# Building the scan's decay matrices by two fp32r products instead of a GpSimd mask and one fp32 product

## The chip, the core and the metric

One core of a Trainium2 chip runs the whole kernel as one program. The metric is device time in microseconds (us) of one execution; the figure of a kernel is the median of its runs. The engines are PE (matrix products), ACT (ScalarE), DVE (VectorE), POOL (GpSimd) and the DMA queue of SP, each with its own instruction stream, kept in step by semaphores.

## What is computed

The reference is one layer of a hybrid decoder for a 528-row prompt (16 meta tokens and 512) and 8 samples of 8 rows, 592 rows in all: a normalisation, one input projection, a Mamba-2 scan with 32 heads in 4 groups of 8, a short gated convolution, a merge, and a mixture of experts. The change lies in the scan. Within a chunk of rows, a head's weights are

```
acum  = cumsum(dt * a_neg)                       # running sum inside the chunk
seg   = acum[l] - acum[s]
decay = exp(where(s <= l, seg, -inf))
wts   = (C B^T)[l, s] * decay * dt[s]
y_diag = wts @ x
```

so each group, chunk and head needs a square matrix of differences of running sums, cut by the causal mask, through an exponential.

## The kernel before

The 592 rows are held as five tiles (`TILES`): four of 128 rows and a last one of 80, which holds the prompt's last 16 rows and the eight samples. The projections are products in fp32r of weights split into a high and a low part; `pe_block` (line 649) issues one 128-column block, either whole (48 products: 24 weight tiles, each times two column halves of 264 and 328) or one half at a time (`part`, 24 products). Each block's weights come through SP's queue (`load_block`, L478), are split by ACT (`split_hi`, L1656) and by POOL (`split_lo`, L1954).

The scan runs over four groups `g`. Every engine's order inside a group is written out by hand. First come the projections and convolutions of the group (DVE L1258 and L1260, ACT L1733 and L1734), then the five tiles `i`. In tile `i`, PE transposes x (L755), forms C B^T (L758) and B's transpose (L759), and makes two banks of decay exponents, `q` = 0 and 1, four heads each (L770). For these POOL has built `rbuf` ahead (`decays`, L2035): for each head the lower mask `m_le` times that tile's `da` column. One fp32 product of the strict mask `m_gt` with `rbuf` sums it up: column c of row s gets the sum of `da` over the rows between s and c. ACT takes the exponential of the whole bank (L1767), DVE multiplies by C B^T, which it has masked on the way out of PSUM (`cbm`, L1280; the product L1285), and PE uses the result at L822. L776 gives the contribution of the carried state, L828 the new state, L846 adds the former. Between the two banks of tiles 1 and 2, and behind L776 of tiles 0 to 2, PE has halves of later projection blocks to do (L649); tiles 3 and 4 have none. Tile 4 has the samples' own states instead: transposes (L787), copies by ACT (L1777) and products (L796).

Waits that matter here: L770 of q = 1 waits until DVE has read the bank of the tile before (`s_u`, L1310); L776 and L787 wait for `cbm` (`s_cb`); L822 waits for both products L1285 (`s_w`).

Ahead of the groups, behind the second turn of a projection loop (`o1_turn`), PE makes the running sums of all tiles (L728 to L732) and ACT their exponentials (L1718 to L1721).

Of the kernel before, what the change touches and what calls it, by code (L numbers as in the profile page):

```python
# [65 lines left out]
def build(nc, ins, outs):  # L66
    ctx = ExitStack()
    with ctx:
        def sem(name):
# [9 lines left out]
        ident = sb("ident", [P, P])  # L79
        m_le = sb("m_le", [P, P])  # L80
        m_gt = sb("m_gt", [P, P])
        ones = sb("ones", [P, P])
# [75 lines left out]
        dt_rows, _ = carve(so + 2 * (WDT + P), [T])  # L158
# [11 lines left out]
        rbuf, o = carve(o, [2, 4 * P])  # L170
        bmask, _ = carve(o - 8 * P, [NSEQ, NST])
# [150 lines left out]
        s_u, s_y1, s_xd, s_cb, s_bt, s_r, s_exp, s_w, s_st = (  # L322
            sem(n) for n in ("s_u", "s_y1", "s_xd", "s_cb", "s_bt", "s_r", "s_exp", "s_w", "s_st"))


        s_dx, p_df, s_df, s_cm, s_bm, hs_in, hs_out, p_h0, s_h0, p_yb, p_hs, s_hd, s_hs = (
            sem(n) for n in ("s_dx", "p_df", "s_df", "s_cm", "s_bm", "hs_in", "hs_out", "p_h0", "s_h0", "p_yb", "p_hs", "s_hd", "s_hs"))
# [328 lines left out]
        def _(pe):  # L656
# [75 lines left out]
            nc.tensor.matmul(pS[0:R4, 0:HEADS], m_blk4[:, :], da[0:R4, 4, :], start=True, stop=True).then_inc(s_cum, 1)  # L732
# [11 lines left out]
            for g in range(GROUPS):  # L744
# [5 lines left out]
                for i in range(TILES):  # L750
                    r = ROWS[i]
                    le, gt = (m_le, m_gt) if i < 4 else (m_le4, m_gt4)
# [366 lines left out]
        def _(dve):  # L1119
# [126 lines left out]
            v.tensor_copy(df[:, :, :].rearrange("p k s -> p (k s)"), pT[:, 0:GROUPS * GK * NSEQ]).then_inc(s_df, 1)  # L1246
            with dve.Fori(0, GROUPS) as g:
# [16 lines left out]
                for i in range(TILES):  # L1264
# [364 lines left out]
        def _(act):  # L1629
# [292 lines left out]
        def _(pool):  # L1922
# [81 lines left out]
            with pool.Fori(0, GROUPS) as g:  # L2004
# [52 lines left out]
                gp.tensor_tensor(bmask[0:R4], btok[0:R4, 0, :].unsqueeze(1).broadcast_to([R4, NSEQ, NST]),  # L2057
                                 m_blk4[:, LASTP:R4:SLEN].unsqueeze(2).broadcast_to([R4, NSEQ, NST]), ALU.mult
                                 ).then_inc(s_bm, 1)

                pool.wait_ge(s_df, 1)
# [148 lines left out]
```

## Time and profile before

| | |
|---|---|
| median of 3 runs | 1302.77 us (1302.36 to 1303.2) |
| the profiled execution | 1305.76 us |
| its span, first to last instruction | 1304.0 us |
| mean granted TensorE clock | 0.969 of full speed |
| PE busy | 1214.8 us (93%) |
| DVE busy | 539.3 us (41%) |
| POOL busy | 466.0 us (36%) |
| ACT busy | 387.9 us (30%) |

The span is what the trace covers; the execution's own time is 1.76 us longer. A busy PE is one with a product in flight; an instruction's end is modelled, so the distance between starts is the better measure of what PE spends on it.

### The profile page before, as it was taken

How to read it: one execution, taken by the hardware profiler on the slowest of the kernel's cores; microseconds unless marked ns; L12 is line 12 of the kernel's file. 1: busy time of each engine (PE TensorE's matmuls, PEld its weight loads, DVE VectorE, ACT ScalarE, POOL GpSimd, SP SyncE). 2: the span in 40 equal slices, each digit the busy share in tenths (PEclk: the TensorE clock that was granted, in tenths of full speed). 3: DMA queues.
4: the chain of work that ended last, by engine and by line, in shares of the span. 5: the costliest groups of instructions: out<-in, count | busy, mean ns of one | idle time of the engine just before them, and what ended most of it. 6: DMA issues, size and time to landing. Idle time of an engine off the chain costs nothing.

```text
span 1304.0 us, 22313 instructions
## 1 busy us (share of the span) xinstructions
PE 1214.8 (93%) x8749; PEld 1045.2 (80%) x8749; DVE 539.3 (41%) x852; ACT 387.9 (30%) x569; POOL 466.0 (36%) x366
## 2 busy tenths in 40 slices
PE   6999999999999999999999989999998879877895
PEld 5999999999985986798598679999997645533562
DVE  5445442002656675485667552004344241120114
ACT  4211114433433533443353262122323110010112
POOL 5444432333444453454445353333430121113110
PEclk8999999998999999999999999999999798998898
DMA  6333322222511720351072122253547999999995
GB/s 158 81 83 79 81 65 65 64 81 65 146 50 31 186 67 17 107 144 49 26 186 72 33 89 81 82 133 110 166 141 302 366 394 403 406 400 396 396 377 175
DMA packets 185455, 207.20 MB, mean 159 GB/s; under 512 B 12646, under 2 KB 162278, under 8 KB 176899
## 3 DMA queue, kind: packets, MB, share of 16 engines
q1 hardware_dynamic: 175506, 187.12, 43.4%
q0 software_dynamic: 6048, 12.54, 3.5%
q10 hardware_dynamic: 3822, 6.39, 1.3%
q8 instruction: 62, 1.02, 0.3%
q14 instruction: 17, 0.13, 0.0%
HBM read 191.56 MB, written 26.05 MB: 167 GB/s over the span
## 4 chain that ended last, share of the span: by engine, by line
PE 77%; DMA 8%; DVE 6%; issue 3%; ACT 2%; POOL 2%; SPq 1%; ACTq 0%; DVEq 0%; POOLq 0%
PE acc L649 48%; PE pTS L1045 6%; PE acc L928 4%; PE acc L1089 3%; DMA area<-in_w_down 2%; DMA area<-in_w_up 2%; DMA ring<-in_w_gate 2%; DVE area L1260 2%; PE pTS L828 2%; PE pY L822 1%; PE pY L846 1%; SPq L574 1%; PE acc L787 1%; PE pO L776 1%; DMA area<-in_w_down,area 1%
## 5 line engine op out<-in xcount | busy, mean ns | idle before, releaser
L649 PE MATMUL acc<-h_parts,ring_parts 128*128 128x328 f32 (+1 forms) x3840 | 549.5, 305 | 6.3 <-DVE area L1305 2.2
L649 PEld LDWEIGHTS acc<-h_parts,ring_parts 128*128 128x128 f32 x3840 | 535.6, 191 | 21.3 <-issue 15.3
L1954 POOL TENSOR_TENSOR ring_parts<-ring,ring_parts 128x1024 fp32r<-128x1024 f32 x112 | 280.6, 2506 | 436.6 <-ACT ring_parts L1656 436.5
L1656 ACT ACTIVATE ring_parts<-ring 128x1024 fp32r<-128x1024 f32 x112 | 118.4, 1058 | 393.8 <-PE acc L649 368.5
L1045 PE MATMUL pTS<-area,big 128*64 128x256 f32 x672 | 107.0, 397 | 11.8 <-DMA ring<-in_w_gate 3.9
L649 PE MATMUL acc<-u_parts,ring_parts 128*128 128x264 f32 (+1 forms) x640 | 109.4, 299 | 0.0
L1045 PEld LDWEIGHTS pTS<-area,big 128*64 128x64 f32 x672 | 68.6, 144 | 41.2 <-issue 9.2
L649 PEld LDWEIGHTS acc<-u_parts,ring_parts 128*128 128x128 f32 x640 | 96.4, 188 | 0.0
L649 PE MATMUL acc<-area_parts,ring_parts 128*128 128x264 f32 (+1 forms) x512 | 91.1, 299 | 0.0
L1260 DVE SCALAR_TENSOR_TENSOR area<-area,xvec 128x616 f32<-128x616 f32 x72 | 84.9, 1179 | 10.5 <-DVE area L1258 0.6
L649 PEld LDWEIGHTS acc<-area_parts,ring_parts 128*128 128x128 f32 x512 | 78.4, 188 | 0.0
L2109 POOL DMA_INDIRECT y_sum<-big,area x17 | 27.0, 1591 | 120.6 <-DVE big L1560 89.2
L1089 PE MATMUL acc<-area,big 128*64 128x512 f32 x168 | 56.9, 663 | 9.8 <-DMA area<-in_w_down 6.3
L2103 POOL DMA_INDIRECT big<-h_rows,area x17 | 17.7, 1040 | 119.8 <-PE acc L1010 87.8
L2035 POOL TENSOR_TENSOR area<-m_le,da 128x512 f32<-128x512 f32 (+1 forms) x40 | 42.7, 1075 | 36.9 <-PE pY L770 21.8
L1045 PE MATMUL pTS<-ring,big 128*64 128x256 f32 x224 | 51.5, 389 | 4.4 <-DMA big<-in_w_gate 2.3
L928 PE MATMUL acc<-h_parts,ring_parts 128*128 128x264 f32 (+1 forms) x384 | 54.8, 301 | 0.0
L1545 DVE TENSOR_TENSOR big<-big,pTS 128x256 f32<-128x256 f32 x17 | 7.2, 421 | 115.0 <-PE pTS L1045 115.0
L1285 DVE TENSOR_TENSOR area<-area 128x512 f32<-128x512 f32 (+1 forms) x40 | 42.3, 1081 | 27.7 <-ACT area L1767 25.8
L1560 DVE TENSOR_SCALAR big<-acc,area 128x1024 f32<-128x1024 f32 x16 | 20.5, 1284 | 79.4 <-PE acc L1089 79.4
L1889 ACT ACTIVATE big<-pTS 128x256 f32<-128x256 f32 x17 | 6.5, 383 | 156.9 <-PE pTS L1045 156.9
L928 PEld LDWEIGHTS acc<-h_parts,ring_parts 128*128 128x128 f32 x384 | 52.7, 188 | 0.0
(380 smaller groups left out, 1517.9 us busy)
## 6 DMA issues: line engine op xcount, KB each, us to landing
ring<-in_w_in SPq DMA_DIRECT2D x80, 512.0 KB, 4.0
area<-in_w_gate SPq DMA_DIRECT2D x20, 1024.0 KB, 19.3
area<-in_w_up SPq DMA_DIRECT2D x20, 1024.0 KB, 21.8
area<-in_w_down SPq DMA_DIRECT2D x20, 1024.0 KB, 18.0
area<-in_state_ssm SPq DMA_DIRECT2D x16, 512.0 KB, 6.9
out<-area SPq DMA_DIRECT2D x16, 512.0 KB, 5.4
ring<-in_w_ssd_out SPq DMA_DIRECT2D x16, 512.0 KB, 4.1
ring<-in_w_gate SPq DMA_DIRECT2D x7, 1024.0 KB, 17.2
```

Of the source, the lines that this page charges most:

```text
L649: m = nc.tensor.matmul(acc[a][:, h, 0:n], w[s][:, k, :], x[:, k, h * HALF:h * HALF + n], start=first and k == 0 and w is w_hi and x is hi, ...
L828: nc.tensor.matmul(pS[:, :], btok[0:kk, i % 2, :], xte[0:kk, i % 2, :], start=True, stop=True).then_inc(p_sn, 1)
L928: m = nc.tensor.matmul(acc[a][:, h, 0:n], w[f % 2][:, k, :], x[:, k, h * HALF:h * HALF + n], start=k == 0 and w is w_hi and x is mT_hi, st ...
L1045: m = nc.tensor.matmul((pT, pS)[part][main_of(j), 0:FE], xT_[:, k, main_of(j)], wexp[(2 * p + j) % UNROLL][part][:, k, :], start=k == 0, s ...
L1089: m = nc.tensor.matmul(acc[1][main_of(j), h, :], hT_main[:, ft, main_of(j)], wexp[(2 * p + j) % UNROLL][2][:, ft, h * 512:(h + 1) * 512], ...
L1260: x = v.scalar_tensor_tensor(o_, raw[:, c % 2, n:n + XCONV], w[:, 0, n:n + 1], o_, ALU.mult, ALU.add)
L1285: v.tensor_tensor(w, w, cbm[0:r, 0:r].unsqueeze(1).broadcast_to([r, 4, r]), ALU.mult).then_inc(s_w, 1)
L1560: v.tensor_scalar(ye_main[p % 2], acc[1].rearrange("p a b -> p (a b)"), gate_main[:, column_of(p):column_of(p) + 1], None, ALU.mult).then_ ...
L1656: a_.activation(w_hi[b % 2], w_raw[b % 2], ACT.Copy).then_inc(hi_done, 1)
L1954: gp.tensor_tensor(w_lo[b % 2], w_raw[b % 2], w_hi[b % 2].bitcast(F32), ALU.subtract).then_inc(lo_done, 1)
L2035: gp.tensor_tensor(rbuf[0:r, q, 0:4 * r].rearrange("p (h c) -> p h c", h=4), le[0:r, 0:r].unsqueeze(1).broadcast_to([r, 4, r]), da[0:r, i, ...
L2109: pool.indirect_dma_start(y_sum[:, :], bass.IndirectOffsetOnAxis(ap=sid_main[:, at:at + 1], axis=0), ye_main[p % 2], None, bounds_check=DU ...
```

## The change

The sums themselves are now made once, ahead of the groups. PE adds five products that put the running sums of 32 heads as rows into PSUM (`xT_new`); ACT copies them to fp32r (`acum_hi`), DVE subtracts to get the rest (`acum_lo`), and SP writes both to DRAM (`acum_rows`). DVE overwrites `da` with the negated running sums, and clears `arow`. For each group SP loads, by five small DMAs (`load_rows`), two rows (high and low) for each tile into `arow`, 128 rows by 8 heads of columns.

In a tile, L770 becomes two fp32r products into the same bank: the identity times a mask `m_neg` (0 or -2^100, the same for four heads, by a broadcast), and a selecting column `pick[:, i]`, broadcast to all output rows, times `arow`: column c of every row gets the running sum at c. The negated running sum of the row is added by ACT as the exponential's bias, which differs by head, so that each bank takes four exponentials of 128 columns instead of one of 512. POOL's `decays` are gone. The mask is in the exponent now, so DVE only copies `cbm`. `bmask` moves into the buffer `raw` and is made by three instructions instead of one; some masks move in memory.

```
-                        pe.wait_ge(s_r, g * 10 + (2 * i + q + 1))
                         if q == 0:
+                            pe.wait_ge(ac_rows, 32 + 16 * TILES * (g + 1))
                             pe.wait_ge(s_exp, g * 10 + (2 * i + 1))
                             pe.wait_ge(s_st, g * 6 + (i + 1))
                         else:
                             pe.wait_ge(s_u, g * 5 + (i + 1))
-                        nc.tensor.matmul(seg_bank(q)[0:r, 0:4 * r], gt[0:r, 0:r], rbuf[0:r, q, 0:4 * r],
-                                         start=True, stop=True).then_inc(p_seg, 1)
+                        sel = pick[:, i:i + 1].broadcast_to([P, r])
+                        far = (m_neg if i < 4 else m_neg4)[0:r, 0:r].unsqueeze(1).broadcast_to([r, 4, r])
+                        nc.tensor.matmul(seg_bank(q)[0:r, 0:4 * r], ident_r[0:r, 0:r], far, start=True, stop=False)
+                        nc.tensor.matmul(seg_bank(q)[0:r, 0:4 * r], sel, arow[:, q * 4 * r:(q + 1) * 4 * r],
+                                         start=False, stop=True).then_inc(p_seg, 1)
...
-                    le = m_le if i < 4 else m_le4
-                    v.tensor_tensor(cbm[0:r, 0:r], pO[0:r, 0:r], le[0:r, 0:r], ALU.mult).then_inc(s_cb, 1)
+                    v.tensor_copy(cbm[0:r, 0:r], pO[0:r, 0:r]).then_inc(s_cb, 1)
...
-                        a_.activation(wts[0:r, q, 0:4 * r], seg_bank(q)[0:r, 0:4 * r], ACT.Exp).then_inc(s_exp, 1)
+                        for h in range(4):
+                            x = a_.activation(wts[0:r, q, h * r:(h + 1) * r], seg_bank(q)[0:r, h * r:(h + 1) * r], ACT.Exp,
+                                              bias=da[0:r, i, bass.ds(g * HPG + 4 * q + h, 1)])
+                        x.then_inc(s_exp, 1)
...
-                def decays(i, q):
-
-                    r = ROWS[i]
-                    le = m_le if i < 4 else m_le4
-                    hold(pool, p_seg, g * 10 + (2 * i + q + 1))
-                    gp.tensor_tensor(rbuf[0:r, q, 0:4 * r].rearrange("p (h c) -> p h c", h=4),
-                                     le[0:r, 0:r].unsqueeze(1).broadcast_to([r, 4, r]),
-                                     da[0:r, i, bass.ds(g * HPG + 4 * q, 4)].unsqueeze(2).broadcast_to([r, 4, r]),
-                                     ALU.mult).then_inc(s_r, 1)
...
+                nc.tensor.matmul(xT_new[0:HEADS, i * P:i * P + r], d_i, le[0:r, 0:r], start=True, stop=True)
...
+            a_.activation(acum_hi, xT_new[0:HEADS, 0:T], ACT.Copy).then_inc(s_dta, 1)
...
+            dve.wait_ge(s_dta, 7)
+            v.tensor_scalar(da.rearrange("p i h -> p (i h)"), pY[:, 0:160], -1.0, None, ALU.mult).then_inc(s_ac, 1)
+            dve.wait_ge(s_dta, 8)
+            v.memset(arow.bitcast(F32), 0.0).then_inc(s_ac, 1)
+            v.tensor_tensor(acum_lo, xT_new[0:HEADS, 0:T], acum_hi.bitcast(F32), ALU.subtract).then_inc(s_ac, 1)
...
+            sp.wait_ge(s_dta, 8)
+            sp.dma_start(acum_rows[0], acum_hi.bitcast(F32)).then_inc(ac_rows, 16)
+            sp.wait_ge(s_ac, 3)
+            sp.dma_start(acum_rows[1], acum_lo.bitcast(F32)).then_inc(ac_rows, 16)
+            def load_rows(g):
+                heads = bass.ds(g * HPG, HPG)
+                for i in range(TILES):
+                    at, r = (32 * i, P) if i < 4 else (2, R4)
+                    sp.dma_start(arow[at:at + 2, 0:HPG * r].bitcast(F32).rearrange("p (h c) -> p h c", c=r),
+                                 acum_rows[:, heads, tok(i)]).then_inc(ac_rows, 16)
+            sp.wait_ge(ac_rows, 32)
+            load_rows(0)
...
+                if not last:
+                    load_rows(g + 1)
...
+            gp.tensor_scalar(m_neg, m_le, FAR, -FAR, ALU.mult, ALU.add)
```

`load_rows(0)` stands in SP's order behind the loop's last weight load and ahead of the first of the groups (`load_cb(0)`); `load_rows(g + 1)` stands behind the four stores of group `g` (L529) and ahead of the next group's weight loads.

## Rows read from the trace of the kernel before

**Rows 1.** The page: the chain that ended last, by engine.

```profile
PE 77%; DMA 8%; DVE 6%; issue 3%; ACT 2%; POOL 2%; SPq 1%; ACTq 0%; DVEq 0%; POOLq 0%
```

**Rows 2.** Third group's tiles: length, then busy PE, PEld, DVE, ACT, POOL; PEclk.

```profile
586.13:647.77 61.64, 58.47 (x391) 41.97 (x392) 35.34 (x63) 22.88 (x39) 28.12 (x19) 1.00 0.11 30
```

**Rows 3.** Timeline, tile 1 of the third group; start, duration, engine, line, what; idle before.

```profile
599.10 0.69 DVE L1285 TENSOR_TENSOR area<-area 128x512 f32<-128x512 f32 x1
...
600.67 1.02 PE L770 MATMUL pY<-area,m_gt 128*128 128x512 f32 x2
...
601.52 1.02 PE L776 MATMUL pO<-area 128*128 128x512 f32 x2
...
606.07 1.09 PE L822 MATMUL pY<-area 128*64 128x128 f32 x16
```

**Rows 4.** Lines L1733, L1734, L1767: duration min/median/max, first and last start, forms.

```profile
L1733 ACT ACTIVATE area<-area,xvec x24: 723/737/745, 331.3 to 698.7; 128x528 f32<-128x528 f32 x24
L1734 ACT ACTIVATE area<-area,xvec x24: 332/333/348, 332.0 to 699.4; 128x64 f32<-128x64 f32 x24
L1767 ACT ACTIVATE area<-pTS x20: 432/597/598, 360.3 to 744.6; 128x512 f32<-128x512 f32 x16, 80x320 f32<-80x320 f32 x4
```

**Rows 5.** Timeline, end of the third group's convolutions and its tile 0.

```profile
580.69 4.26 DVE L1260 SCALAR_TENSOR_TENSOR area<-area,xvec 128x616 f32<-128x616 f32 x3
580.69 2.59 POOL L2035 TENSOR_TENSOR area<-m_le,da 128x512 f32<-128x512 f32 x2
585.10 0.74 ACT L1733 ACTIVATE area<-area,xvec 128x528 f32<-128x528 f32 x1 [6.03 <-DVE area L1260]
585.74 0.33 ACT L1734 ACTIVATE area<-area,xvec 128x64 f32<-128x64 f32 x1
...
586.13 0.66 PE L755 MATMUL pTS<-ident,area 128*128 128x128 f32 x4 [0.41 <-ACT area L1734]
...
587.81 1.28 ACT L1767 ACT_TABLE_LOAD   x1
...
593.24 1.09 PE L822 MATMUL pY<-area 128*64 128x128 f32 x16
```

**Rows 6.** Line L1260 of DVE over the run.

```profile
L1260 DVE SCALAR_TENSOR_TENSOR area<-area,xvec x72: 859/862/2779, 319.8 to 697.7; 128x616 f32<-128x616 f32 x72
```

**Rows 7.** Timeline, tile 3 of the third group.

```profile
623.61 0.60 ACT L1767 ACTIVATE area<-pTS 128x512 f32<-128x512 f32 x1 [0.58 <-PE pTS L770]
...
624.66 1.12 PE L776 MATMUL pO<-area 128*128 128x512 f32 x2 [0.21 <-DVE area L1280]
...
624.73 1.85 DVE L1285 TENSOR_TENSOR area<-area 128x512 f32<-128x512 f32 x2
...
626.68 1.09 PE L822 MATMUL pY<-area 128*64 128x128 f32 x16 [0.90 <-issue]
```

**Rows 8.** Timeline, tile 4 of the third group.

```profile
632.42 1.94 PE L787 MATMUL acc<-ident,area 128*128 128x128 f32 x16 [0.55 <-DVE area L1280]
...
633.09 2.07 ACT L1777 ACTIVATE area<-acc 128x512 f32<-128x512 f32 x4 [0.74 <-PE acc L787]
```

**Rows 9.** Timeline: POOL near the start, and ACT behind L1721.

```profile
12.58 5.15 POOL L1960 TENSOR_TENSOR h_parts<-big,h_parts 128x1024 fp32r<-128x1024 f32 x2 [7.61 <-ACT h_parts L1661]
...
229.96 1.28 ACT L1656 ACT_TABLE_LOAD   x1 [7.47 <-PE acc L649]
```

**Rows 10.** Timeline: SP's issues ahead of the groups and behind the third, ACT's split.

```profile
279.48 0.37 SPq L478 DMA_DIRECT2D ring<-in_w_sc_out  x1
287.28 32.10 SPq L478 DMA_DIRECT2D ring<-in_w_in  x5
...
653.37 13.24 SPq L478 DMA_DIRECT2D ring<-in_w_in  x3
...
662.61 1.06 ACT L1656 ACTIVATE ring_parts<-ring 128x1024 fp32r<-128x1024 f32 x1 [1.36 <-PE acc L649]
```

**Rows 11.** The page: the weight blocks' loads, KB each, median us from issue to landing.

```profile
ring<-in_w_in SPq DMA_DIRECT2D x80, 512.0 KB, 4.0
```

More of the change, by code:

```diff
@@ L48 @@
 EPS = 1e-6
+FAR = 2.0 ** 100
 TAIL = XH * (1 + NSEQ)
@@ L76, in bank @@
             return ctx.enter_context(nc.psum_tensor(name, shape, F32))[tuple(slice(None) for _ in shape)]
[L79 to L82, printed above, removed]
+        ident_r = sb("ident", [P, P], F32R)
+        ident = ident_r.bitcast(F32)
+        m_neg = sb("m_neg", [P, P], F32R)
+        ones_r = sb("ones", [P, P], F32R)
+        ones = ones_r.bitcast(F32)
         R4 = ROWS[4]
         m_le4 = sb("m_le4", [R4, R4])
-        m_gt4 = sb("m_gt4", [R4, R4])
         m_blk4 = sb("m_blk4", [R4, R4])
+        m_neg4 = sb("m_neg4", [R4, R4], F32R)
+        pick = sb("pick", [P, TILES], F32R)
         eps = sb("eps", [P, 1])
@@ L157, in build @@
         wdt_hi, wdt_lo = (area_parts[:, so + n * (WDT + P):so + (n + 1) * (WDT + P)] for n in range(2))
-        dt_rows, _ = carve(so + 2 * (WDT + P), [T])
+        dt_rows, mo = carve(so + 2 * (WDT + P), [T])
+        m_gt, mo = carve(mo, [P])
+        m_le, mo = carve(mo, [P])
+        m_gt4 = carve(mo, [R4])[0][0:R4, :]
+        at_pad = so - 4 * SPAD
+        acum_hi, acum_lo = (area_parts[0:HEADS, at_pad + n * 2 * SPAD:at_pad + n * 2 * SPAD + T] for n in range(2))
         dx = v2
@@ L169, in build @@
         cv, o = carve(o, [2, XPAD])
-        rbuf, o = carve(o, [2, 4 * P])
-        bmask, _ = carve(o - 8 * P, [NSEQ, NST])
+        arow = area_parts[:, o:o + HPG * P]
+        o += HPG * P
+        bmask = [raw[:, n, XH:XH + 4 * NST].rearrange("p (s n) -> p s n", n=NST) for n in range(2)]
         wts, o = carve(o, [2, 4 * P])
@@ L270, in build @@
                       [acc[1][:, h, :] for h in range(2)], [acc[0][:, h, :] for h in range(2)]]
+        acum_rows = nc.dram_tensor("acum_rows", [2, HEADS, T], F32).ap()
         def expert_slot(u):
@@ L320, in build @@
         p_xt, p_cb, p_seg, p_yo, p_y, p_sn, p_yt = (sem(n) for n in ("p_xt", "p_cb", "p_seg", "p_yo", "p_y", "p_sn", "p_yt"))
[L322 to L327, printed above, removed]
+        s_u, s_y1, s_xd, s_cb, s_bt, s_ac, s_exp, s_w, s_st = (
+            sem(n) for n in ("s_u", "s_y1", "s_xd", "s_cb", "s_bt", "s_ac", "s_exp", "s_w", "s_st"))
+        s_dx, p_df, ac_rows, s_cm, s_bm, hs_in, hs_out, p_h0, s_h0, p_yb, p_hs, s_hd, s_hs = (
+            sem(n) for n in ("s_dx", "p_df", "ac_rows", "s_cm", "s_bm", "hs_in", "hs_out", "p_h0", "s_h0", "p_yb", "p_hs", "s_hd", "s_hs"))
         p_so, so_out, s_uz, s_sq, p_gn, s_rm, s_so = (
@@ L412, in hs_tiles @@
             last = (pT, pO)[k % 2]
-            return ((slice(32, 64), slice(2, 6), acc[k % 2][:, 1, :]), (slice(0, 32), slice(0, 2), acc[k % 2][:, 0, 256:512]),
-                    (slice(64, R4), slice(6, 8), last[:, 0:256]))
+            return ((slice(32, 64), bmask[0], acc[k % 2][:, 1, :]), (slice(0, 32), bmask[1][:, 0:2], acc[k % 2][:, 0, 256:512]),
+                    (slice(64, R4), bmask[1][:, 2:4], last[:, 0:256]))
         def conv_tile(turn, c):
@@ L731, in _ @@
                                  start=True, stop=True)
-            nc.tensor.matmul(pS[0:R4, 0:HEADS], m_blk4[:, :], da[0:R4, 4, :], start=True, stop=True).then_inc(s_cum, 1)
+                nc.tensor.matmul(xT_new[0:HEADS, i * P:i * P + r], d_i, le[0:r, 0:r], start=True, stop=True)
+            nc.tensor.matmul(pS[0:R4, P:P + HEADS], m_blk4[:, :], da[0:R4, 4, :], start=True, stop=True).then_inc(s_cum, 1)
             with pe.Fori(2, 8) as f:
@@ L834, in state_update @@
                         def state_update(k):
-                            for rows, seqs_, out in hs_tiles(k):
-                                m = nc.tensor.matmul(out, xte[rows, 0, k * P:(k + 1) * P], bmask[rows, seqs_, :],
+                            for rows, mask, out in hs_tiles(k):
+                                m = nc.tensor.matmul(out, xte[rows, 0, k * P:(k + 1) * P], mask[rows],
                                                      start=True, stop=True)
@@ L1245, in _ @@
             dve.wait_ge(p_df, 1)
-            v.tensor_copy(df[:, :, :].rearrange("p k s -> p (k s)"), pT[:, 0:GROUPS * GK * NSEQ]).then_inc(s_df, 1)
+            v.tensor_copy(df[:, :, :].rearrange("p k s -> p (k s)"), pT[:, 0:GROUPS * GK * NSEQ]).then_inc(s_dx, 1)
             with dve.Fori(0, GROUPS) as g:
@@ L1720, in _ @@
             a_.activation(dec[:, :, :], pY[:, 320:480].rearrange(f3, h=HEADS), ACT.Exp).then_inc(s_dta, 1)
-            a_.activation(sdec[:, :], pS[0:R4, 0:HEADS], ACT.Exp).then_inc(s_dta, 1)
+            a_.activation(sdec[:, :], pS[0:R4, P:P + HEADS], ACT.Exp).then_inc(s_dta, 1)
+            a_.activation(acum_hi, xT_new[0:HEADS, 0:T], ACT.Copy).then_inc(s_dta, 1)
             with act.Fori(2, 8) as f:
@@ L1932, in _ @@
             gp.memset(eps[:, :], EPS)
-            link(gp.memset(ident[:, :], 0.0))
+            link(gp.memset(ident, 0.0))
             def select(out, in_, pattern, base, mult, op=ALU.is_ge, fill=0.0):
@@ L1937, in select @@
                                       channel_multiplier=mult))
-            select(ident[:, :], ident[:, :], [[-1, P]], 0, 1, ALU.not_equal, 1.0)
+            select(ident_r, ident, [[-1, P]], 0, 1, ALU.not_equal, 1.0)
             select(m_le[:, :], m_le[:, :], [[1, P]], 0, -1)
@@ L1954, in split_lo @@
                 gp.tensor_tensor(w_lo[b % 2], w_raw[b % 2], w_hi[b % 2].bitcast(F32), ALU.subtract).then_inc(lo_done, 1)
+            pick_ = pick.bitcast(F32)
+            link(gp.memset(pick_, 0.0))
+            link(gp.memset(pick_[0:4, 4:5], 1.0))
+            link(gp.memset(pick_[0:2, 4:5], 0.0))
+            for i in range(4):
+                link(gp.memset(pick_[32 * i:32 * i + 2, i:i + 1], 1.0))
+            pool.wait_ge(consts, 1)
+            gp.tensor_scalar(m_neg, m_le, FAR, -FAR, ALU.mult, ALU.add)
+            gp.tensor_scalar(m_neg4, m_le4[:, :], FAR, -FAR, ALU.mult, ALU.add)
             gp.memset(wdt_hi[:, WDT:WDT + P].bitcast(F32), 0.0)
@@ L2056, in _ @@
                 hold(pool, p_seg, g * 10 + 12)
[L2057 to L2061, printed above, removed]
+                for first, to in ((2, bmask[0]), (0, bmask[1][:, 0:2]), (6, bmask[1][:, 2:4])):
+                    mine = to[0:R4]
+                    ends = m_blk4[:, LASTP:R4:SLEN][:, first:first + mine.shape[1]]
+                    x = gp.tensor_tensor(mine, btok[0:R4, 0, :].unsqueeze(1).broadcast_to(mine.shape),
+                                         ends.unsqueeze(2).broadcast_to(mine.shape), ALU.mult)
+                x.then_inc(s_bm, 1)
+                pool.wait_ge(s_dx, 2)
                 hold(pool, p_h0, g * 8 + 8)
```

5 lines of the change are left out of this document (removed).

## The prediction

> **What bounds the kernel now.** I read the chain that ended last first: PE holds 77% of it, DVE 6%, ACT and POOL 2% each [rows 1]. The reader is to see that POOL's masks, which the change removes, are hardly on it as work; what counts is what PE spends in the scan and where it stands still there. Next the busy times of a group's five tiles: of 61.64 us PE is busy for 58.47, at full granted clock, and the other engines for less than 36 each [rows 2]. So in most of a tile a shorter product shortens the run, and in a few places it only makes a longer gap. The timeline says which. I read the third group, which the other three repeat.
>
> In tiles 0 to 2 PE never waits once the tile has begun: a half of a projection block follows L776 and covers the exponentials and DVE's products, up to L822 at 606.07 [rows 3]. In tile 3 there is no such half. PE stands before L776 (0.21 us) and before L822 (0.90 us); DVE's two products L1285 end at 624.73 + 1.85 = 626.58 and L822 starts at 626.68 [rows 7]: there ACT and DVE set the end. In tile 4 PE stands 0.55 us before L787, which waits for DVE's L1280 [rows 8]: there it is DVE's work on the tile before, which no product here precedes. And at the head of the group PE stands 0.41 us for ACT's last convolution, which waited 6.03 us for DVE's L1260 [rows 5].
>
> **The products on PE.** Today an fp32 product of 512 columns takes 601.52 - 600.67 = 0.85 us from its start to the next (two passes, x2) [rows 3]; I use 0.86, 0.43 a pass. The trace has no fp32r product of 512 columns. The nearest are the halves in fp32r: behind L776, which occupies PE until about 601.52 + 0.86 = 602.38, 24 products of 328 columns have PE until L822 starts at 606.07 [rows 3]: 154 ns each, 0.47 ns a column, so 240 ns for 512. Two of them take 0.48 us: a saving of 0.38 us a bank. Bounds: at 2.4 GHz, the full granted clock of [rows 2], one column a cycle, 512 columns take 213 ns (saving 0.43); with a pass as dear as the fp32 pass of 0.43 us the saving is 0. I take 0.38, because L649's products are of the very kind. The Trainium skill ("TensorE: Matmul & The Clock Gate", section on the back-to-back issue gap) gives N / 2.4 GHz plus about 2.5 ns, an estimate of 216 ns here, less than these rows show; by it the forecast would be about 1 us lower.
>
> Tiles 0 to 2 have six banks a group: 6 x 0.38 = 2.3 us, all on PE's path if their cover holds. Four groups: 9.2 us.
>
> **The exponentials on ACT.** A bank's exponential takes 597 ns now. With a bias from memory, 528 columns take 737 ns and 64 take 333 (L1733, L1734) [rows 4]: 0.87 ns a column, so 0.39 us for 128. L1734 starts 0.64 us after an L1733 that lasts 0.74 [rows 5]: followers overlap by about 0.09, and four cost 4 x 0.30 + 0.09 = 1.3 us a bank instead of 0.6. Bounds: 0.30 each when they overlap, 0.39 when they don't. I take 0.30. The work that hides it in tiles 1 and 2 is the half block of 3.7 us behind L776. Tile 0 has the same half: there ACT loads a table until 587.81 + 1.28 = 589.09 [rows 5]; the load moves 0.7 earlier (next part), so eight exponentials end at 588.4 + 2.5 = 590.9 and DVE's last product of 0.69 us [rows 3] at 591.6, while L822 comes at 593.24 [rows 5] - 0.41 - 0.76 = 592.07. Covered, by 0.5 us.
>
> Tile 3 has no cover. PE's first bank is ready 0.38 us earlier, so ACT starts at 623.23 instead of 623.61 [rows 7]; eight exponentials end at 623.23 + 8 x 0.30 + 0.09 = 625.72; DVE's last product, 0.69 without POOL beside it, ends at 626.45, and L822 follows at 626.55 instead of 626.68: 0.1 us gained a group, where PE alone would have gained 0.76. What is late here next is ACT. Tile 4: L787 waits for DVE, so PE's shorter products gain nothing; ACT's eight exponentials of 80 columns (0.26 each) begin at about 630.8 and end at 632.9, before L1777 starts at 633.09 [rows 8]. So 0, by a margin of 0.2 us. Queued behind them on ACT are L1777's copies, and PE's products with the samples' states wait for those. Four groups, both tiles: 0.4 us gained.
>
> **POOL's decays.** Removed: two run beside DVE's last L1260 (580.69, 2.59 us for two) [rows 5]. The three L1260 there take 4.26 us, while the same instruction takes 0.86 at its shortest and at its median [rows 6]: about 1.3 us less for three with their waits between. The convolution ends that much earlier, ACT's chain up to the table load gains 0.7 or more, and PE's 0.41 us are gone, in the three groups that show this wait: 1.2 us. Bounds 0 (if POOL's work was not what slowed L1260) and 1.2. I take 1.2, since POOL's two and DVE's first start together at 580.69. DVE's `cbm` as a copy instead of a product reads the same 128 columns: nothing. `bmask` in three instructions has the whole of tile 4 as its cover, since only the products that end the tile read it.
>
> **What is added ahead of the groups.** PE: five fp32 products of 128 columns, a quarter of 0.86 each: 1.0 us, on the path. The lower bound is 0.3, if the weight loads beside them hide them; I take 1.0. ACT's copy of 592 columns (under 0.8 us) and DVE's three instructions lie in a stretch in which ACT then stands 7.47 us for PE [rows 9]. POOL's memsets and masks lie in its idle 7.61 us [rows 9]. SP: two writes, the wait for their landing, five issues of loads. Between its issues at 279.48 and 287.28 SP stands for 7.4 us [rows 10]; seven issues at 0.37 and a landing no longer than the 4.0 of a whole weight block [rows 11] make 6.6, so it is hidden, and 1 us over would still only delay a weight load by that.
>
> **load_rows in the groups.** Five issues of 0.37 us at most [rows 10], 1.9 us, go ahead of the weight load at 653.37. That load's data is split by ACT at 662.61, when ACT had waited for PE, not for data [rows 10]; with the 4.0 us of landing [rows 11] it is there at 659.3. Hidden by 3 us; without cover each us over it would come three times.
>
> **The sum.** 9.2 + 0.4 + 1.2 - 1.0 = 9.8 us less than the profiled 1305.76, so 1295.9 (span 1294.2); that execution lay 3 us above the median, so against the median 1302.77 - 9.8 = 1293.0. What follows the scan is started by its end and carries the gain on. Its own range: 0.43 a bank and 0.3 for the prologue give 12 us, 0.32 a bank and no relief for DVE give 7: 1290.5 to 1296.
>
> **Rivals.** *Small exponentials don't overlap.* Then each costs 0.39 (0.35 in tile 4). Tile 3: 623.23 + 3.1 + 0.1 + 0.7 = 627.1, a loss of 0.45; tile 0 loses 0.15; tile 4: 633.55 against 633.09, 0.46. 9.8 - 0.4 - 4 x 1.06 = 5.2 us gained: 1297.6. For it: the biased rows here come in pairs only. Against: in those pairs the second starts before the first's end. The Trainium skill ("Advanced Engine Details and Errata", section The Read-Write Bubble) speaks for it: memory latency is exposed between a ScalarE engine's instructions, and tiles of 512 or more are advised, which is what the change gives up. That start before the end shows the bubble only in part.
>
> *The broadcast operands, or fp32r at 512 columns, are no cheaper than fp32.* Saving per bank 0. Tile 3 then loses 0.25 a group, the head's 1.2 and the prologue's 1.0 cancel: 1303.6, no change. For it: no row shows either form. Against: L649's 0.465 ns a column.
>
> *ACT becomes the bound (the other side).* Each exponential names a column by the group's register. If this makes the distance 0.50 us instead of 0.30, tile 3's L822 comes at 623.23 + 4.0 + 0.1 + 0.75 = 628.1 (1.4 later), tile 0 loses 1.1, tile 4 1.5: 4 x 4.0 = 16 against 9.2 + 1.2 - 1.0: 6.6 us slower, 1309.4. It decides from about 0.43 us on, where the loss of a group reaches its gain of 2.35. Against: L1733 takes its bias by the same register and its pair shows 0.09 overlap.
>
> *More than forecast.* Products at 213 ns, hidden prologue, and DVE's shorter products L1285 taking 0.3 more out of each tile 3: 10.3 + 0.4 + 1.2 + 1.2 - 0.3 = 12.8 us, 1290.0.
>
> **Chances.** Forecast 0.60, no overlap 0.16, more 0.10, no cheaper 0.07, ACT the bound 0.07. The range of 8 in 10 takes the first three, down to 1288 and up to 1300. What can be told from no change is 0.2%, 2.6 us: below 1300.2 is faster. Faster 0.86, same 0.07, slower 0.07.
>
> **What would show it.** L770's two products 0.24 us apart; L1767's exponentials 0.30 us apart and about 0.39 long; 12.83 - 0.76 = 12.07 us from tile 0's L822 to tile 1's (593.24 to 606.07 now); L822 of tile 3 waiting for DVE almost as late as before; L787 of tile 4 still waiting for L1280; no wait of L755 for L1734; L1260 at 580.69 without stretch. The prediction is wrong if exponentials lie 0.4 us apart or more, if PE waits in tiles 1 and 2, or if weights come late behind `load_rows`.

## The result, and the profile after

The changed kernel takes 1294.47 us (median of 6 runs, 1293.87 to 1298.84) against 1302.62 us before (6 runs, 1302.01 to 1305.45): 0.994 of it, 95% interval 0.9926 to 0.9953, 8.15 us less. The forecast was 1293.0 (1288.0 to 1300.0), faster.

| | before | after |
|---|---|---|
| profiled execution, its span (us) | 1305.76, 1304.0 | 1294.7, 1293.0 |
| mean granted TensorE clock | 0.969 | 0.973 |
| PE busy (us) | 1214.8 | 1199.7 |
| DVE busy (us) | 539.3 | 522.7 |
| POOL busy (us) | 466.0 | 428.1 |
| ACT busy (us) | 387.9 | 410.7 |

The chain that ended last, by engine, as [rows 1]:

```profile
PE 80%; DMA 8%; DVE 4%; issue 3%; POOL 2%; ACT 2%; SPq 1%; ACTq 0%; DVEq 0%; POOLq 0%
```

DVE's share fell from 6% to 4% and PE's rose from 77% to 80%; ACT's stayed at 2% although it has 22.8 us more to do.

Where the time came from is best read as the distance from one tile's first transposes (L755, now L783) to the next tile's. Tile 4 is counted up to the transposes of the carried state (L852, now L883), and the "head" runs from there to the first transposes of the next group's tile 0, over that group's projections. All four groups agree within 0.03 us but for one head before (56.56, see the end).

| us | tile 0 | tile 1 | tile 2 | tile 3 | tile 4 | head (3 of them) | ahead of the groups |
|---|---|---|---|---|---|---|---|
| before | 9.99 | 12.83 | 12.83 | 7.79 | 15.14 | 55.07 | |
| after | 9.84 | 12.06 | 12.06 | 7.42 | 15.16 | 54.53 | |
| gained | 0.15 | 0.77 | 0.77 | 0.37 | -0.02 | 0.54 | -1.9 |
| forecast | 0.76 | 0.76 | 0.76 | 0.10 | 0 | 0.40 | -1.0 |

4 x 2.04 + 3 x 0.54 - 1.9 = 7.9 us, against 8.15 measured. The 1.9 is worked out under the second experiment.

The timeline of tile 0, third group, after (start, duration, engine, line, what; idle before and its releaser); it answers to [rows 5]:

```profile
574.61 2.88 DVE L1296 SCALAR_TENSOR_TENSOR area<-area,xvec 128x616 f32<-128x616 f32 x3
...
577.63 0.74 ACT L1769 ACTIVATE area<-area,xvec 128x528 f32<-128x528 f32 x1 [4.63 <-DVE area L1296]
...
579.51 0.60 PE L783 MATMUL pTS<-ident,area 128*128 128x128 f32 x4
...
580.17 0.27 PE L787 MATMUL pO<-ident,area 128*128 128x128 f32 x1
...
580.20 0.48 PE L800 MATMUL pTS<-m_neg,ident 128*128 128x512 f32 x1
580.26 0.69 DVE L1311 TENSOR_TENSOR area<-pTS,dt 128x512 f32<-128x512 f32 x1 [2.77 <-PE pTS L783]
...
580.52 0.39 PE L801 MATMUL pTS<-area_parts,pick 128*128 128x512 f32 x1
...
580.75 0.40 PE L800 MATMUL pY<-m_neg,ident 128*128 128x512 f32 x1
...
580.87 0.68 DVE L1312 TENSOR_TENSOR area<-pTS,dte 128x512 f32<-128x512 f32 x1
580.98 0.40 PE L801 MATMUL pY<-area_parts,pick 128*128 128x512 f32 x1
...
581.46 0.28 DVE L1315 COPY area<-pO 128x128 f32<-128x128 f32 x1
...
581.80 1.12 PE L807 MATMUL pO<-area 128*128 128x512 f32 x2 [0.42 <-DVE area L1315]
```

Three things stand here. The three L1296 take 2.88 us instead of 4.26, and L783 no longer waits for ACT: the head's gain. The products follow each other after 0.23 us (580.52, 580.75, 580.98), where an fp32 product took 0.85; the first of a bank behind the transposes takes 0.32, but starts 0.03 us after L787's transpose instead of 0.11. And L807 waits 0.42 us for DVE's copy `cbm`, which comes third on DVE, behind `xdt` (L1311) and `xte` (L1312): tile 0's gain is held up here.

Tile 3, as [rows 7], and the start of tile 4, as [rows 8]:

```profile
615.01 1.15 ACT L1804 ACTIVATE area<-pTS,da 128x128 f32<-128x128 f32 x4 [0.29 <-PE pTS L801]
...
616.03 1.16 ACT L1804 ACTIVATE area<-pY,da 128x128 f32<-128x128 f32 x4
616.35 1.12 PE L807 MATMUL pO<-area 128*128 128x512 f32 x2 [0.67 <-DVE area L1315]
616.42 1.50 DVE L1320 TENSOR_TENSOR area<-area 128x512 f32<-128x512 f32 x2
...
618.02 1.09 PE L853 MATMUL pY<-area 128*64 128x128 f32 x16 [0.54 <-issue]
...
623.72 1.96 PE L818 MATMUL acc<-ident,area 128*128 128x128 f32 x16 [0.82 <-DVE area L1315]
623.79 1.51 DVE L1320 TENSOR_TENSOR area<-area 80x320 f32<-80x320 f32 x2
624.50 2.07 ACT L1816 ACTIVATE area<-acc 128x512 f32<-128x512 f32 x4 [0.49 <-PE acc L818]
```

PE's gain in tile 3 shows again as its wait before L807 (0.67 us, 0.21 before), and in tile 4 before L818 (0.82, 0.55 before). The view of L1804's groups gives the exponentials:

```profile
L1804 ACT ACTIVATE area<-pTS,da x80: 312/368/382, 360.2 to 733.9; 128x128 f32<-128x128 f32 x64, 80x80 f32<-80x80 f32 x16
```

0.37 us is the median of one, near the forecast 0.39; four take 1.15 us, so they start (1.15 - 0.37) / 3 = 0.26 us apart.

### The profile page after: what moved, and what is told of

Same layout as the page of the kernel before. It is cut to its first block, busy times and chain, and to the rows that moved or that the text cites. A ratio compares the mean times of both kernels' runs of the same rounds, so it can differ in the third digit from the quotient of the medians.

```text
span 1293.0 us, 22479 instructions
## 1 busy us (share of the span) xinstructions
PE 1199.7 (93%) x8759; PEld 1040.4 (80%) x8759; DVE 522.7 (40%) x855; ACT 410.7 (32%) x690; POOL 428.1 (33%) x343
## 4 chain that ended last, share of the span: by engine, by line
PE 80%; DMA 8%; DVE 4%; issue 3%; POOL 2%; ACT 2%; SPq 1%; ACTq 0%; DVEq 0%; POOLq 0%
PE acc L677 52%; PE pTS L1076 6%; PE acc L959 4%; PE acc L1120 3%; DMA area<-in_w_down 2%; DMA area<-in_w_up 2%; DMA ring<-in_w_gate 2%; PE pTS L859 2%; PE pY L853 2%; PE pY L877 1%; SPq L602 1%; PE pO L807 1%; PE acc L818 1%; DMA area<-in_w_down,area 1%; PE pO L827 1%
## 5 line engine op out<-in xcount | busy, mean ns | idle before, releaser
L677 PE MATMUL acc<-h_parts,ring_parts 128*128 128x328 f32 (+1 forms) x3840 | 543.1, 303 | 6.3 <-DVE area L1340 2.2
L1296 DVE SCALAR_TENSOR_TENSOR area<-area,xvec 128x616 f32<-128x616 f32 x72 | 79.4, 1102 | 10.5 <-DVE area L1294 0.6
L1120 PE MATMUL acc<-area,big 128*64 128x512 f32 x168 | 54.2, 639 | 7.6 <-DMA area<-in_w_down 4.2
L1076 PE MATMUL pTS<-big 128*64 128x256 f32 x192 | 44.4, 390 | 1.0 <-DMA area<-in_w_down,area 1.0
L1236 DVE TENSOR_TENSOR big<-acc,area 128x528 f32 (+1 forms) x8 | 5.7, 708 | 91.9 <-PE acc L677 91.9
```

Of the source, the lines that this page charges most:

```text
L677: m = nc.tensor.matmul(acc[a][:, h, 0:n], w[s][:, k, :], x[:, k, h * HALF:h * HALF + n], start=first and k == 0 and w is w_hi and x is hi, ...
L1076: m = nc.tensor.matmul((pT, pS)[part][main_of(j), 0:FE], xT_[:, k, main_of(j)], wexp[(2 * p + j) % UNROLL][part][:, k, :], start=k == 0, s ...
L1120: m = nc.tensor.matmul(acc[1][main_of(j), h, :], hT_main[:, ft, main_of(j)], wexp[(2 * p + j) % UNROLL][2][:, ft, h * 512:(h + 1) * 512], ...
L1296: x = v.scalar_tensor_tensor(o_, raw[:, c % 2, n:n + XCONV], w[:, 0, n:n + 1], o_, ALU.mult, ALU.add)
```

## The experiments

All start from the changed kernel. Ratios are against the kernel before, run beside them: it took 1302.4 us (median of 11 runs) beside e1, e2, e5 and e6, and 1304.1 us (17 runs) beside e3, e4, e7 and e8, so totals are compared by their ratios, 0.994 for the changed kernel. What one edit does is read from the lengths above, which repeat within an execution to 0.04 us, but for one head each in the kernel before and in e4, and for the heads of e8.

**1. Is it DVE's order that holds up tile 0? (e1_cbm_first)**

```
                     v.tensor_tensor(xdt[0:r, i % 2, :].rearrange(byhead, c=HD), x_i, per_head(dt_), ALU.mult)
-                    v.tensor_tensor(xte[0:r, i % 2, :].rearrange(byhead, c=HD), x_i, per_head(dte), ALU.mult
-                                    ).then_inc(s_xd, 1)
                     dve.wait_ge(s_bt, g * 5 + (i + 1))
                     v.tensor_copy(cbm[0:r, 0:r], pO[0:r, 0:r]).then_inc(s_cb, 1)
+                    v.tensor_tensor(xte[0:r, i % 2, :].rearrange(byhead, c=HD), x_i, per_head(dte), ALU.mult
+                                    ).then_inc(s_xd, 1)
```

> The changed kernel with one DVE step moved: the copy cbm goes between the products xdt and xte instead of behind both. Nothing is left out. Theory: in tile 0 PE's shorter bank products only ran into the wait for cbm, so L807 now starts as soon as PE is free, 0.6 us earlier, and L853 with it: 4 x 0.6 = 2.4 us faster than the changed kernel, about 1292.1. Tile 3's L807 also starts earlier but its L853 stays, set by ACT's exponentials; tile 4's L818 stays, because it also waits for xte. Rival 1: tile 0 is held by ACT's exponentials behind the table load; then nothing changes (1294.5). Rival 2: DVE also sets the end of tile 3; then another 0.5 us a group, about 1290.

Measured 1290.63 us (1289.19 to 1298.62), ratio 0.9913 (0.9891 to 0.9936). Tile 0 takes 9.25 us, 0.59 less, and PE runs through (its timeline):

```profile
581.56 0.40 PE L801 MATMUL pY<-area_parts,pick 128*128 128x512 f32 x1
581.79 1.11 PE L807 MATMUL pO<-area 128*128 128x512 f32 x2
```

Tile 3 stays at 7.42: L807's wait is gone, and the one before L853 grew from 0.54 to 1.1 us, so there ACT and DVE set the end whatever PE does. Tile 4 lost 0.12 (15.28), since L818 also waits for `xte` (`s_xd`), which now comes last. The tiles make it 4 x (0.59 - 0.12) = 1.9 us; the two totals' intervals overlap. Tile 0's lost gain is shown to be this wait: it now takes 9.25 us, where the forecast's saving gives 9.99 - 0.76 = 9.23.

**2. Do the five new products cost so much because they stand between others? (e2_sums_grouped)**

```
-                nc.tensor.matmul(xT_new[0:HEADS, i * P:i * P + r], d_i, le[0:r, 0:r], start=True, stop=True)
+            for i in range(TILES):
+                r = ROWS[i]
+                nc.tensor.matmul(xT_new[0:HEADS, i * P:i * P + r], da[0:r, i, :], (m_le if i < 4 else m_le4)[0:r, 0:r],
+                                 start=True, stop=True)
```

> The changed kernel with the five products that put the running sums into rows moved behind the fifteen others instead of one behind each three. Nothing is left out. Theory: a product with a stationary of 32 columns between products with stationaries of 128 columns keeps weight loads from overlapping, so that each costs 0.45 us instead of the 0.22 of its own two passes; grouped, the stretch shortens by about 1.1 us, to about 1293.4. Rival: each product costs 0.45 wherever it stands: no change in the stretch. The clock, which falls to half near the end of this stretch in both kernels, may hide part of it: the stretch's first three tiles are compared.

Measured 1293.57 us (1291.67 to 1295.04), ratio 0.9923 (0.9911 to 0.9935): not to be told from the changed kernel by its total. The timeline of the changed kernel shows a round of four products 1.12 us after the last one, at full clock; in e2 a round of the three old ones follows after 0.67:

```profile
218.98 0.41 PE L756 MATMUL pY<-da,area 128*128 128x32 f32 x2
...
219.76 0.41 PE L760 MATMUL pTS<-area,da 128*32 128x128 f32 x2
220.10 0.41 PE L756 MATMUL pY<-da,area 128*128 128x32 f32 x2
```

So a new product costs 0.45 us there. The weight loads (PEld) show where half of it goes: ahead of a new product, and of the old one behind it, the load starts 0.20 us after the product before has started (218.64 against 218.44, 218.98 against 218.77), among the old ones 0.08. Grouped, they are 0.42 apart (1.67 us for four, e2's timeline), but at half the clock, which fell just then (0.58 from 221 to 222 us, then 0.50):

```profile
221.08 1.87 PE L762 MATMUL pTS<-area,da 128*32 128x128 f32 x8
222.75 0.47 PE L762 MATMUL pTS<-m_le,da 80*32 80x80 f32 x2
```

To take out the clock I measured from the first of these products to the first tile, and took off (1 - granted clock) x 16 us for the two stretches in which it falls, 218 to 234 and 300 to 316. The windows of the changed kernel (busy time of the engines, then granted clock, DMA share, GB/s):

```profile
218.00:234.00 16.00, 16.00 (x99) 14.48 (x99) 4.14 (x7) 4.30 (x8) 2.35 (x1) 0.79 0.15 44
...
300.00:316.00 16.00, 16.00 (x125) 16.00 (x124) 2.38 (x5) 4.83 (x7) 5.65 (x5) 1.00 0.25 67
```

It has 357.39 - 217.96 - 0.21 x 16 = 136.07 us; before 357.35 - 218.05 - (0.11 + 0.21) x 16 = 134.2; e2 356.43 - 217.77 - (0.11 + 0.11) x 16 = 135.14. The five products cost 1.9 us as the change has them and 0.9 grouped. This leans on the granted clock as the windows give it, in two digits (0.01 is 0.16 us). The other six executions with the products as the change has them (e1, e3 to e6, e8) give 135.8 to 136.3 by the same sum, and e7, where they are grouped, 135.1. One case needs no such sum. In e5 the clock stayed up until these products were over (1.00 from 220 to 222 us, 0.97 from 222 to 224), as it did before; the first product and the block behind them, before and in e5:

```profile
218.05 0.30 PE L728 MATMUL pY<-da,m_le 128*128 128x32 f32 x2
...
221.52 8.32 PE L649 MATMUL acc<-h_parts,ring_parts 128*128 128x264 f32 x48
```

```profile
217.71 0.30 PE L756 MATMUL pY<-da,area 128*128 128x32 f32 x2
...
223.24 8.31 PE L677 MATMUL acc<-h_parts,ring_parts 128*128 128x264 f32 x48
```

5.53 us against 3.47: 2.06 us for the five. Grouped products at the full clock stand in no trace.

**3. What does a pair of the new products cost on the path? (e3_banks_twice)** Each pair runs twice; the second writes the same values.

```
+                        for again in range(2):
...
+                        m.then_inc(p_seg, 1)
```

> The changed kernel with each bank's pair of fp32r products issued twice into the same bank; the second pair begins anew, so nothing is left out. A pair takes 0.46 us in the trace of the changed kernel. Theory (only the tiles whose end PE sets pay): tiles 1 and 2 grow by 0.92 us each, from 12.06 to 12.98; tile 0 by 0.3, because 0.6 of its time is a wait for cbm; tile 3 by about 0.46, the delay of ACT's first exponential; tile 4 by nothing, since L818 waits for DVE. 2.6 us a group, 10.4 in all, about 1305. Rival (PE sets every tile): ten pairs a group, 4.4 us a group, about 1312.

Measured 1307.17 us (1302.28 to 1309.26, 10 runs), ratio 1.0021 (1.0006 to 1.0035). The tiles take 10.07, 12.96, 12.99, 7.88 and 15.16 us: 0.23, 0.90, 0.93, 0.46 and 0 more, 2.5 a group. Two pairs add 0.9 us where PE is the bound, 0.23 a product; had PE set every tile, as the rival has it, they would have added 4.4 a group. Most of tile 0's 0.92 goes into its wait for `cbm` (0.59 by e1), tile 3 grows by one pair, as expected from the delay of ACT's first exponential, and tile 4, which waits for DVE, by nothing. The tiles give 10.1 us; by the ratios the total lies 1.0021 - 0.994 = 0.0081 of the kernel before, 10.6 us, above the changed kernel's.

**4. Do the small exponentials cost anything? (e4_one_exp)** One exponential of 512 columns a bank, as before; it leaves out the bias, so the decays are other numbers.

```
-                        for h in range(4):
-                            x = a_.activation(wts[0:r, q, h * r:(h + 1) * r], seg_bank(q)[0:r, h * r:(h + 1) * r], ACT.Exp,
-                                              bias=da[0:r, i, bass.ds(g * HPG + 4 * q + h, 1)])
-                        x.then_inc(s_exp, 1)
+                        a_.activation(wts[0:r, q, 0:4 * r], seg_bank(q)[0:r, 0:4 * r], ACT.Exp).then_inc(s_exp, 1)
```

> The changed kernel with one exponential of 512 columns for a bank, without the bias; this leaves the row's running sum out of the decay, so its output isn't the reference's. Theory: the split into four costs ACT about 0.55 us a bank, and only tile 3 pays, because DVE's copies and products are due there almost as late: 0.2 us a group, 0.8 in all, about 1293.7; tiles 0, 1, 2 and 4 keep their lengths of 9.84, 12.06, 12.06 and 15.16. Rival (ACT is what tile 3 waits for, as the prediction had it): tile 3 shortens by about 0.9, from 7.42 to 6.5, 3.6 us in all.

Tile 3 takes 7.23 us, 0.19 less; tiles 0, 1, 2 and 4 are as in the changed kernel (9.84, 12.06, 12.06, 15.14). The total, 1286.34 us (ratio 0.9867, 0.9846 to 0.9887), says nothing of this: with other decays other numbers reach the experts, and from the last group's tile 4 to the end its profile has 553.1 us against 561.0. So four exponentials with a bias in place of one without cost 0.19 x 4 = 0.8 us in the whole kernel, in tile 3 alone. The rival (0.9 us a group) is out.

**5. Is the head's gain POOL's? (e5_pool_back)** POOL gets two products of the shape of the old `decays` back beside the last L1296, into a buffer that is overwritten later; POOL waits for each of them, and DVE, ahead of its next use of that buffer in tile 0, for both.

```
+                    if i == 0:
+                        dve.wait_ge(s_ac, g * 2 + 5)
...
+                for n in range(2):
+                    gp.tensor_tensor(ytok.rearrange("p (h c) -> p h c", h=4), ones.unsqueeze(1).broadcast_to([P, 4, P]),
+                                     da[:, 0, bass.ds(g * HPG + 4 * n, 4)].unsqueeze(2).broadcast_to([P, 4, P]), ALU.mult
+                                     ).then_inc(s_ac, 1)
+                    pool.wait_ge(s_ac, g * 2 + (4 + n))
```

> The changed kernel with two POOL products of 128x512 put back where the first two decays stood, into a buffer that is overwritten later; their result is not used. Theory: what freed the head of a group was POOL's absence beside DVE's last L1296, so these stretch again from 2.9 to about 4.3 us, and PE waits 0.4 us again ahead of the first transposes in three groups: 1.2 us slower, about 1295.7. Rival: DVE's instructions did not suffer from POOL, the head got shorter for another reason: no change, 1294.5.

The head is 55.07 us again, and its timeline shows the whole chain of [rows 5] back:

```profile
576.92 4.27 DVE L1296 SCALAR_TENSOR_TENSOR area<-area,xvec 128x616 f32<-128x616 f32 x3
576.92 1.04 POOL L2081 TENSOR_TENSOR area<-ones,da 128x512 f32<-128x512 f32 x1
...
578.14 1.38 POOL L2081 TENSOR_TENSOR area<-ones,da 128x512 f32<-128x512 f32 x1 [0.18 <-POOL area L2081]
...
582.37 0.66 PE L783 MATMUL pTS<-ident,area 128*128 128x128 f32 x4 [0.42 <-ACT area L1772]
```

DVE's three instructions take 4.27 us with POOL beside them and 2.88 without; 0.54 us at each of the three heads reach the end. The total was 1296.22 us (1292.95 to 1296.79), ratio 0.9941 (0.9927 to 0.9954); it does not show these 1.6 us, the length of the heads does.

**6. Tile 4 as well (e6_cbm_xd):** e1's order, and L818's wait for `xte` left out, which these transposes don't use.

```
-                        pe.wait_ge(s_xd, g * 5 + 5)
```

> As the kernel with cbm ahead of xte, and in tile 4 the state transposes L818 no longer wait for xte (the later wait for it stays). Nothing is left out. Theory: in tile 4 L818 is held by DVE's work on the tile, not by PE or ACT; it starts 0.6 us earlier, and ACT's copies L1816 then begin when its exponentials are done, 0.45 us earlier: 1.8 us faster than with cbm first alone, about 1290.3. Rival: ACT's eight exponentials set tile 4 already; then no more than 0.1 us a group.

Measured 1291.43 us (1286.38 to 1292.27), ratio 0.9903 (0.9887 to 0.9919). Tile 4 takes 14.56 us, 0.60 less than in the changed kernel; the others are as in e1. The totals of e1 and e6 can't be told apart; the lengths say 4 x (0.59 + 0.60) = 4.8 us less than the changed kernel. The rival, 0.1 us a group at most, is out.

**7. Both mends together (e7_best):** e6 and the grouped products.

> All three edits together: cbm ahead of xte, L818 without its wait for xte, the five products of running sums grouped. Nothing is left out. Theory: 1.2 us a group from the first two, as seen in the tile lengths (9.24 and 14.56 instead of 9.84 and 15.16), and about 1 us from the grouping at the full granted clock: 4.8 + 1 below the changed kernel, about 1288.7. Rival for the grouping: a product costs 0.42 us grouped too, and only the tiles' 4.8 us are gained, about 1289.7. If the clock stays at its full level in the stretch with the grouped products, their spacing (0.21 or 0.42 us) decides.

Measured 1289.43 us (1287.01 to 1292.85), ratio 0.9896 (0.9877 to 0.9916): faster than before by 1.0% and, by the ratios, than the changed kernel by 0.994 - 0.9896 = 0.0044, 5.7 us. Its tiles are e6's (9.23, 12.05, 12.05, 7.42, 14.56). The clock fell in the grouped products again (0.50 from 221 us on), so their spacing at the full clock was not seen; the sum of experiment 2 (135.1) speaks for the theory.

**8. How much room has `load_rows`? (e8_rows_twice)** A second small DMA, DRAM to DRAM, behind each of its five.

```
                     sp.dma_start(arow[at:at + 2, 0:HPG * r].bitcast(F32).rearrange("p (h c) -> p h c", c=r),
                                  acum_rows[:, heads, tok(i)]).then_inc(ac_rows, 16)
+                    sp.dma_start(acum_copy[:, heads, tok(i)], acum_rows[:, heads, tok(i)]).then_inc(ac_rows, 16)
```

> The changed kernel with five more small DMAs in each load of the running sums' rows, from DRAM to DRAM, issued between the five that are needed; nothing is left out. Theory: SP issues the next weight loads some 4 us later once more in three groups, ACT's split then waits for data, but the split rows are due only 4 us after that, so PE doesn't see it: no change, 1294.5. Rival: the weight loads are at their limit already; PE stands up to 3.5 us in three groups: about 1303.

The expectation of no change fell: the heads are 55.70, 55.55 and 55.35 us instead of 54.53, 3.0 us in all. The total, 1297.2 us (1294.55 to 1298.25), ratio 0.9943 (0.9921 to 0.9965), is too wide to show them. SP's loads and ACT's split at the first head, first in the changed kernel, then in e8:

```profile
427.49 8.50 SPq L489 DMA_DIRECT2D ring<-in_w_in  x3
...
431.83 1.06 ACT L1691 ACTIVATE ring_parts<-ring 128x1024 fp32r<-128x1024 f32 x1 [1.33 <-PE acc L677]
```

```profile
431.93 8.30 SPq L490 DMA_DIRECT2D ring<-in_w_in  x3
...
436.09 1.06 ACT L1693 ACTIVATE ring_parts<-ring 128x1024 fp32r<-128x1024 f32 x1 [5.08 <-DMA ring<-in_w_in]
```

In e8 ACT waits for the data, which lands 436.09 - 431.93 = 4.16 us after its issue. In the changed kernel the same 4.16 end at 431.65, and ACT, which waits for PE, starts at 431.83: 0.2 us of room there (at the third head 0.6: 649.22 + 4.16 = 653.38, and ACT starts at 653.96). Behind ACT some 3 us more are left: the load comes 4.4 us later in e8, and PE waits 0.9 us, for POOL's split of that block, which the changed kernel does not show (the waits of PE in that stretch, e8):

```profile
PE acc L679 <- POOL ring_parts L1995: 0.9, 1, 0.9
```

## Why the prediction was right, point by point

**The products: right.** 0.24 us forecast, 0.23 measured; e3 gives the same on the path. From L822 of tile 0 to that of tile 1 it is 12.07 us, the figure forecast:

```profile
586.47 1.09 PE L853 MATMUL pY<-area 128*64 128x128 f32 x16
...
598.54 1.09 PE L853 MATMUL pY<-area 128*64 128x128 f32 x16
```

Stationary operand, mask and broadcasts add nothing: the rival of products no cheaper than fp32 is out. The Trainium skill ("TensorE: Matmul & The Clock Gate", section on the back-to-back issue gap) gives N / 2.4 GHz plus about 2.5 ns for a product by itself, an estimate of 216 ns. The trace has 230.

**Tiles 0 to 2, 9.2 us: the step that failed.** They gave 4 x (0.15 + 0.77 + 0.77) = 6.8. The forecast asked for tile 0 only whether the exponentials stay covered; they do. It did not ask what L776 waits for. In tiles 1 and 2 a half block stands between the banks, and `cbm` is long done; in tile 0 the two banks are all that stands ahead of L776. The timeline of before, third group, shows how close it was:

```profile
588.13 0.28 DVE L1280 TENSOR_TENSOR area<-pO,m_le 128x128 f32<-128x128 f32 x1
588.67 1.02 PE L776 MATMUL pO<-area 128*128 128x512 f32 x2
```

`cbm` was done at 588.13 + 0.28 = 588.41, 0.26 us ahead of L776, with no wait in the row to give it away. Only 0.25 of 0.76 us could come out, and a 0.1 longer way to L853 (4.67 us from L807, 4.57 before; e1, without the wait, has 4.68, so its cause is open) left 0.15. e1 shows it: 0.59 us come back by moving one instruction.

**Tiles 3 and 4, 0.4 us: right in kind, too small.** ACT and DVE set tile 3's end as forecast, and tile 4 gained nothing. The term that was mis-sized is the distance of the exponentials: 0.26 us and not 0.30. From tile 3's first transposes, at 613.47, the last one ends after 616.03 + 1.16 - 613.47 = 3.72 us; the forecast's 625.72 lies 3.95 behind the transposes of before (621.77, by the lengths); the difference of 0.23 is nearly all of what tile 3 gained beyond the forecast (0.37 against 0.10). So the rival of no overlap is out, and ACT as the bound with it: the column named by a register shows no such delay. The Trainium skill ("Advanced Engine Details and Errata", section The Read-Write Bubble) advises tiles of 512 or 1024 elements. Here e4 puts the price of the shorter ones, bias included, at 0.19 us a group.

**POOL's decays, 1.2 us: right, a little small** (3 x 0.54 = 1.6). e5 shows the cause. All of it lies at the one wait: up to the last products of the block ahead of it the third heads of before and after agree within 0.03 us. The row's 0.41 counts from the modelled end of a product, so the wait was worth more than it says.

**Ahead of the groups, -1.0 us: mis-sized.** A quarter of an fp32 product of 512 columns each was the term; between products of 32 columns each cost 0.45 us, together 1.9 to 2.1. Only grouped does the term hold (0.9, by experiment 2's sum). No row shows the lower bound of 0.3.

**`load_rows`, hidden by 3 us: right in the sum, wrong in its terms.** Five issues take 4.36 us there, not 1.9; the weight load starts 649.22 - 644.38 = 4.8 us behind the last store, where before it started 0.3 behind (stores to 649.07 + 4.01 = 653.08, load at 653.37 [rows 10]). The stores before, then SP's rows after:

```profile
649.07 4.01 SPq L529 DMA_DIRECT2D out<-area  x4
```

```profile
640.41 3.97 SPq L555 DMA_DIRECT2D out<-area  x4
644.58 4.36 SPq L521 DMA_DIRECT2D area_parts<-acum_rows  x5
649.22 8.75 SPq L489 DMA_DIRECT2D ring<-in_w_in  x3
```

That leaves ACT 0.2 to 0.6 us, and e8 shows that some 3 us more lie behind it.

The misses are -2.4 us in tiles 0 to 2, -0.9 ahead of the groups, +1.0 in tiles 3 and 4 and +0.4 at the heads: together -1.9, where the time measured was 1.5 us above the forecast. So the mechanism held where the signs were named: exponentials nearer than 0.4 us, no wait of PE in tiles 1 and 2, no weights late. That the total came so near is in part luck: 1.4 us of the misses went the other way.

## What to carry to other kernels

Where a shorter product is credited to a stretch, look at each wait behind it, not only at the one that is known to be long: a releaser that was done 0.26 us early is the new bound once 0.76 us are saved. Then ask whether the order on the releasing engine has to be so; one moved line gave back more here than tile 0 had gained. And cost a step by the stretch it stands in: a product among small ones, or a small DMA in a loop, cost twice and more what the nearest row of another place said.

## What the runs showed of the hardware that was not expected

**The clock falls behind the small products, and not alike in each execution.** Windows of the changed kernel and of the one before (granted clock in the third column from the end):

```profile
222.00:224.00 2.00, 2.00 (x10) 1.42 (x11) 0.00 (x0) 0.00 (x0) 0.00 (x0) 0.50 0.30 92
224.00:226.00 2.00, 2.00 (x10) 1.77 (x11) 0.33 (x1) 1.15 (x5) 0.00 (x0) 0.50 0.60 178
226.00:228.00 2.00, 2.00 (x10) 2.00 (x10) 1.58 (x3) 0.14 (x1) 0.00 (x0) 0.50 0.00 0
```

```profile
222.00:224.00 2.00, 2.00 (x11) 2.00 (x10) 1.55 (x2) 0.49 (x4) 0.00 (x0) 0.55 0.37 100
...
226.00:228.00 2.00, 2.00 (x17) 2.00 (x16) 0.00 (x0) 0.00 (x0) 0.00 (x0) 1.00 0.00 0
```

In nine of the ten profiled executions (all but e4) PE's clock fell to its lower level (1.2 GHz, 0.50) during or just behind the small products ahead of the groups, while PE stayed busy, and in seven of the ten again from 300 to 316 us, during or behind the small products L738, now L767 (0.53 and 0.50 from 304 to 310 before; 1.00 throughout after). One such fall costs 1.8 to 3.4 us (0.11 or 0.21 x 16). How many an execution has differs: over 218 to 234 and 300 to 316 us the granted clocks were 0.89 and 0.79 before, 0.79 and 1.00 after, 1.00 and 0.89 in e4. The one head of 56.56 us before (55.07 else) lies in a stretch of granted clock 0.91 (520 to 540 us), where the other nine profiles have 1.00; e4's one long head (56.05) lies in one of 0.91 too (410 to 430 us). What makes the difference is left open. It is one reason why two profiles can differ by more than an edit gives, and why the edits were read from tile lengths.

**A small DMA's issue depends on where it stands.** The five of `load_rows` take 1.50 us ahead of the groups and 4.36 inside their loop, with the same sizes; the register in their addresses and the place differ. The trace says more: ahead of the groups each of the five takes 0.26 to 0.28 us, and at the third head they take 1.53, 0.94, 0.67, 0.24 and 0.24, the rest being short steps between them. The last two name the same register and cost no more than ahead of the groups, so the register alone does not make an issue long; the long ones are those that come first behind the four stores. Why these are long was not tried.
